# Mixed-branch diffusion step on one core: Fourier branch by even and odd halves, gate sigmoids in the z eviction, head statistics inside the mLSTM

## What is computed

```python
z = h @ w_in + b_in                    # 6672 columns: q k v o | u | g_a g_b | gates
# branch A: bidirectional mLSTM, 4 heads of 256; hsum = forward + backward
hn = (hsum - mean) * rsqrt(var + eps) * g_head          # per head and token
y_a = (sigmoid(o) * hn) @ w_a
# branch B: 4 groups of 128 channels
uf = u.reshape(B, L, 4, 128)
y_f = real(fft2(uf, axes=(1, 3), norm="ortho"))
y_b = y_f.reshape(B, L, 512) @ w_b
merged = sigmoid(g_a) * y_a + sigmoid(g_b) * y_b
x = layer_norm(ALPHA * x + gate1 * (merged @ w_out))
# then a mixture of 16 experts, top 2, and a second layer norm
```

## Times and profile before

| | |
|---|---|
| Time, median of 3 runs | 1269.01 us (1265.07 to 1269.72) |
| Profiled execution: span, first to last instruction | 1264.4 us (its time outside the span is not listed) |
| PE busy | 1124.0 us (89%) |
| PEld busy | 901.4 us (71%) |
| DVE busy | 693.0 us (55%) |
| ACT busy | 466.9 us (37%) |
| POOL busy | 168.1 us (13%) |
| DMA | 217.00 MB, mean 172 GB/s |
| Chain that ended last | PE 65%, DMA 14%, DVE 13%, ACT 4%, issue 3% |

### The profile page before, as it was taken

The page is one execution under the profiler, slowest core; times in us unless marked ns, Lnnn a source line. Parts: engine busy times, 40 slices in busy tenths (PEclk is TensorE's granted clock), DMA queues, the critical chain, the costliest instruction groups (busy, mean ns, idle before and its releaser), DMA issues.

```text
span 1264.4 us, 15216 instructions
## 1 busy us (share of the span) xinstructions
PE 1124.0 (89%) x5699; PEld 901.4 (71%) x5700; DVE 693.0 (55%) x982; ACT 466.9 (37%) x549; POOL 168.1 (13%) x126
## 2 busy tenths in 40 slices
PE   5899999999999969999989999938999999999710
PEld 1498889999999964767555558826888778778510
DVE  0499982222222224657333319762478988988548
ACT  1431222222222234217211000123478878888522
POOL 3000000000000000000001117510011221122056
PEclk9899999999999999999999999958999999999865
DMA  9644632223222521003311223324769999999542
GB/s 321 237 164 163 216 121 68 66 68 98 66 66 69 180 67 68 1 1 112 161 67 67 83 81 136 138 78 166 266 243 384 398 389 390 393 395 397 213 182 83
DMA packets 110442, 217.00 MB, mean 172 GB/s; under 512 B 3245, under 2 KB 43425, under 8 KB 110401
## 3 DMA queue, kind: packets, MB, share of 16 engines
q1 hardware_dynamic: 103221, 191.67, 42.3%
q0 software_dynamic: 4592, 15.40, 3.5%
q10 hardware_dynamic: 2592, 9.44, 1.8%
HBM read 194.95 MB, written 21.55 MB: 171 GB/s over the span
## 4 chain that ended last, share of the span: by engine, by line
PE 65%; DMA 14%; DVE 13%; ACT 4%; issue 3%; SPq 1%; POOL 0%; POOLq 0%; DVEq 0%; ACTq 0%
PE bank L895 14%; PE bank L896 13%; PE bank L897 13%; DMA z<-w_gate 11%; PE bank L1113 7%; PE bank L1056 2%; DVE g_hl L1527 2%; PE bank L1086 2%; PE bank L1038 2%; DVE z L1291 2%; PE bank L1058 2%; PE bank L1115 2%; ACT g_hl L775 2%; PE bank L886 2%; DMA r<-w_ada 2%
## 5 line engine op out<-in xcount | busy, mean ns | idle before, releaser
L895 PE MATMUL bank<-hT_hi,w_hl 128*128 128x320 f32 x832 | 258.5, 311 | 1.1 <-DVE w_hl L1247 1.1
L896 PE MATMUL bank<-hT_lo,w_hl 128*128 128x320 f32 x832 | 257.1, 309 | 0.0
L897 PE MATMUL bank<-hT_hi,w_hl 128*128 128x320 f32 x832 | 255.2, 307 | 0.0
L895 PEld LDWEIGHTS bank<-hT_hi,w_hl 128*128 128x128 f32 x832 | 156.6, 188 | 7.3 <-issue 5.2
L897 PEld LDWEIGHTS bank<-hT_hi,w_hl 128*128 128x128 f32 x832 | 156.6, 188 | 0.0
L896 PEld LDWEIGHTS bank<-hT_lo,w_hl 128*128 128x128 f32 x832 | 156.3, 188 | 0.0
L1334 DVE TENSOR_TENSOR z<-bank,cols 128x320 f32<-128x320 f32 (+1 forms) x52 | 25.3, 487 | 183.4 <-PE bank L897 183.4
L643 ACT ACTIVATE w_hl<-r 128x1024 fp32r<-128x1024 f32 x52 | 55.0, 1059 | 143.2 <-PE bank L897 143.2
L1527 DVE TENSOR_TENSOR g_hl<-z,g_hl 128x2048 fp32r<-128x2048 f32 x32 | 72.0, 2288 | 34.4 <-ACT g_hl L775 34.4
L565 POOL TENSOR_TENSOR z<-z 128x640 f32<-128x640 f32 x8 | 18.0, 2250 | 527.2 <-DVE z L1470 527.2
L1113 PE MATMUL bank<-z,r 128*128 128x512 f32 x192 | 85.1, 593 | 1.1 <-DVE z L1455 1.1
(11 more groups left out here) (287 smaller groups left out, 2053.2 us busy)
## 6 DMA issues: line engine op xcount, KB each, us to landing
z<-w_gate SPq DMA_DIRECT2D x16, 2048.0 KB, 12.0
z<-w_up SPq DMA_DIRECT2D x16, 2048.0 KB, 11.4
z<-w_down SPq DMA_DIRECT2D x16, 2048.0 KB, 11.7
r<-w_in SPq DMA_DIRECT2D x26, 1024.0 KB, 5.3
z<-w_ada SPq DMA_DIRECT2D x8, 2048.0 KB, 8.0
y_d<-r ACTq DMA_DIRECT2D x18, 512.0 KB, 6.4
r<-w_ada SPq DMA_DIRECT2D x3, 2048.0 KB, 15.6
y_d<-zeros SPq DMA_DIRECT2D x1, 4608.0 KB, 19.6
```

Of the source, the lines that this page charges most:

```text
L895: MM(dst, sta(0), mov(0), start=start, stop=False)
L896: MM(dst, sta(0), mov(1), start=False, stop=False)
L897: return MM(dst, sta(1), mov(0), start=False, stop=stop)
```

## The change

- The position transform of a real signal is even in its cosine part and odd in its sine part. The changed kernel computes the cosine part for 257 of 512 positions (`HALF`) and the sine part for 255 (`ODD`) and mirrors them after the projection with w_b, since that projection acts on channels alone. The channel transform is halved in the same way: 65 cosine and 63 sine columns per group, in one matmul of 128 columns, and the rows of w_b are folded to match (near plus far rows for the even part, far minus near for the odd one). The 64th channel of each group has rows of its own (`wb_mid`, `four_mid`, 4 partitions). The host gives w_b with the far rows in reversed order.
- PE no longer waits for the last unit outputs before the channel transform.
- In the projection to z, ACT evicts both halves of the blocks o, g_a, g_b with a sigmoid; the three sigmoid passes after the mLSTM go.
- DVE takes the statistics of a head right after its second direction (and of the context after the context part), normalises head by head, folds w_b between heads 1 and 2, and gates the transposed blocks in between.
- w_b comes as four loads of 64 partitions, the middle rows in a fifth, behind w_a. The load of x_prompt into r3 moves behind the last gating, since `yb_mix` uses its place.
- ACT copies the first 257 columns of the w_b product out of PSUM (`yb_mix`) and DVE adds and subtracts the other 255 to give both halves.
- Semaphores of the root (`var_ready`, `std_ready`) are shared by three places.

```diff
+    t128 = np.concatenate([np.cos(a[:, 0:65]), np.sin(a[:, 1:64]), np.cos(a), np.sin(a)], 1) / np.sqrt(P)
+    b = 2 * np.pi * ((np.arange(TL)[:, None] * np.arange(HALF)[None]) % TL) / TL
...
+        four_a = zf[:, 0:NT * NG * P].rearrange("p (t c g f) -> p t c g f", t=NT, g=NG, c=2)
...
+        wb_near = r1[:, 0:2048].rearrange("p (n d) -> p n d", n=2)
+        wb_far = r1[:, 2048:4096].rearrange("p (n d) -> p n d", n=2)
+        wb_even = wb_near
+        wb_spare = r1[:, 4096:5120]
+        wb_odd = [r1[:, 3072:4096], r1[:, 2048:3072]]
+        yb_mix = [r3[:, 4096 + s * 512:4608 + s * 512] for s in range(2)]
...
+            wb_rows = a["w_b"][0].rearrange("(n g f) d -> g f n d", n=2, g=2)
+            for g in range(2):
+                sp.dma_start(wb_near[64 * g:64 * g + 64, :, :], wb_rows[g, 0:64]).then_inc(wb_loaded, 16)
+                sp.dma_start(wb_far[64 * g:64 * g + 64, :, :], wb_rows[g, 64:128]).then_inc(wb_loaded, 16)
+            sp.dma_start(wa_sb, a["w_a"][0].rearrange("(k p) n -> p k n", p=P)).then_inc(wa_loaded, 16)
+            sp.wait_ge(four_a_out, NT)
+            sp.dma_start(wb_mid, a["w_b"][0].rearrange("(g f) d -> g f d", g=NG)[:, 64, :]).then_inc(four_loaded, 16)
...
+            sp.wait_ge(y_gated, KT)
             sp.dma_start(xr[:, NL, :], a["x_prompt"][0]).then_inc(xr_loaded, 16)
...
+                    if not gate:
+                        first_half.then_inc(z_out, 1)
+                    else:
+                        act.wait_ge(w_used, 4 * b + f + 1)
+                        A(z[:, bass.ds(4 * b + f, 1), TH:T].rearrange("p a t -> p (a t)"), bank[2 * (f % 2) + 1][:, 0:TH], ACT.Sigmoid,
+                          bias=cols[:, bass.ds(16 + 4 * b + f, 1)]).then_inc(z_out, 1)
...
-            for f in (ZO, ZGA, ZGB):
-                A(z[:, f:f + 8, :], z[:, f:f + 8, :], ACT.Sigmoid).then_inc(sig_ready, 1)
...
+            A(four_p[:, 0, :], bank[2][:, 0:HALF], ACT.Copy).then_inc(four_out, 1)
...
+            A(four_mid[:, :], bank[7][0:NG, 0:HALF], ACT.Copy).then_inc(four_out, 1)
...
+                A(yb_mix[m % 2][:, 0:HALF], bank[YR[m % 2]][:, 0:HALF], ACT.Copy).then_inc(yb_copied, 1)
...
+                for g in range(NG):
+                    last = MM(bank[tt % 2][:, g * P:(g + 1) * P], z[:, ZU + g, tt * P:(tt + 1) * P], t128_sb[:, 0:P], start=True, stop=True)
+                last.then_inc(four_a_mm, 1)
+            pe.wait_ge(four_a_out, NT)
+
+            def pair(s, kind, n):
+
+                return four_a[:, s, kind, 2 * n:2 * n + 2, :].rearrange("p g f -> p (g f)")
+
+            def even(dst, n):
+                for s in range(NL):
+                    last = MM(dst, pair(s, 0, n), four_l[:, 0, s, :], start=(s == 0), stop=(s == NL - 1))
+                return last
...
+            def odd(dst, n):
+                for s in range(NL):
+                    last = MM(dst, pair(s, 1, n), four_l[:, 1, s, 1:HALF - 1], start=(s == 0), stop=(s == NL - 1))
...
+            even(bank[2][:, 0:HALF], 0).then_inc(four_mm, 1)
+            odd(bank[3][:, 0:ODD], 0).then_inc(four_mm, 1)
+            even(bank[4][:, 0:HALF], 1).then_inc(four_mm, 1)
+            for n in range(2):
+                MM(bank[1][:, n * P:(n + 1) * P], pair(NL, 0, n), cos_c, start=True, stop=True)
+            for n in range(2):
+                last = MM(bank[1][:, (2 + n) * P:(3 + n) * P], pair(NL, 1, n), sin_c, start=True, stop=True)
+            last.then_inc(four_mm, 1)
...
+            odd(bank[0][:, 0:ODD], 1)
+            for n in range(2):
+                last = MM(bank[0][:, (2 + n) * P:(3 + n) * P], pair(NL, 1, n), cos_c, start=True, stop=True)
+            last.then_inc(four_mm, 1)
+            pe.wait_ge(unit_out, 30)
+            for s in range(NL):
+                last = MM(bank[7][0:NG, 0:HALF], four_a[:, s, 1, :, 0:1].rearrange("p g o -> p (g o)"), four_l[:, 0, s, :], start=(s == 0), stop=(s == NL - 1))
+            last.then_inc(four_mm, 1)
+
             pe.wait_ge(unit_out, 32)
...
+            pe.wait_ge(four_out, 8)
             TB = ((6, 7), (4, 5))
             for k in range(KT):
-                pe.wait_ge(hn_ready, 1)
+                pe.wait_ge(hn_ready, k // 2 + 1)
...
+            pe.wait_ge(wb_folded, 5)
+            pe.wait_ge(four_loaded, 48)
...
+                for n in range(2):
+                    MM(bank[bb][:, 0:HALF], wb_even[:, n, w], four_p[:, n, :], start=(n == 0), stop=False)
+                MM(bank[bb][:, 0:HALF], wb_mid[:, w], four_mid[:, :], start=False, stop=True)
+                for n in range(2):
+                    MM(bank[bb][:, HALF:TL], wb_odd[n][:, w], four_q[:, n, :], start=(n == 0), stop=(n == 1))
+                for n in range(2):
+                    MM(bank[bc][:, P:2 * P], wb_even[:, n, w], four_pc[:, n, :], start=(n == 0), stop=False)
+                for n in range(2):
+                    MM(bank[bc][:, P:2 * P], wb_odd[n][:, w], four_qc[:, n, :], start=False, stop=(n == 1))
...
+                y_b(m, bc, bb)
+                if m == 0:
+                    pe.wait_ge(wa_loaded, 16)
+                for k in range(KT):
+                    if m == 0:
+                        pe.wait_ge(yin_ready, k + 1)
+                    MM(bank[ba][:, :], wa_sb[:, k, m * P:(m + 1) * P], z[:, ZO + k, 0:TL], start=(k == 0), stop=(k == KT - 1))
...
+            def row_stats(cells):
+
+                for tt, h in cells:
+                    last = V.bn_stats(bn[:, 4 * tt + h, :], hsum[:, tt, h * HD:(h + 1) * HD])
+                then(last)
...
+            row_stats([(NL, h) for h in range(H)])
...
+                if q % 2 == 1:
+                    dve.wait_ge(unit_out, 4 * q + 4)
+                    row_stats([(tt, q // 2) for tt in range(NL)])
...
+            normed(0)
+            normed(1)
+            dve.wait_ge(wb_loaded, 16 * 4)
+            dve.wait_ge(pool_setup, 10)
+            for n in range(2):
+                V.scalar_tensor_tensor(out=wb_spare if n == 0 else wb_odd[1], in0=wb_near[:, n, :], scalar=neg_keep[:, 0:1], in1=wb_far[:, n, :], op0=ALU.mult, op1=ALU.add).then_inc(wb_folded, 1)
+                dve.wait_ge(wb_folded, 2 * n + 1)
+                V.scalar_tensor_tensor(out=wb_even[:, n, :], in0=wb_far[:, n, :], scalar=row_keep[:, 0:1], in1=wb_near[:, n, :], op0=ALU.mult, op1=ALU.add).then_inc(wb_folded, 1)
+                dve.wait_ge(wb_folded, 2 * n + 2)
+            V.tensor_copy(wb_odd[0], wb_spare).then_inc(wb_folded, 1)
+            gated(0)
+            gated(1)
+            normed(2)
+            gated(2)
+            gated(3)
+            normed(3)
+            for k in range(4, KT):
+                gated(k)
...
+                dve.wait_ge(yb_copied, m + 1)
+                V.tensor_tensor(mix[:, TL - 1:HALF - 1:-1], mix[:, 1:HALF - 1], bank[bb][:, HALF:TL], ALU.subtract).then_inc(dve_chain, 1)
+                chain[0] += 1
+                then(V.tensor_tensor(mix[:, 1:HALF - 1], mix[:, 1:HALF - 1], bank[bb][:, HALF:TL], ALU.add))
+                V.tensor_tensor(z[:, ZGA + m, 0:TL], z[:, ZGA + m, 0:TL], bank[ba][:, :], ALU.mult)
+                V.tensor_tensor(z[:, ZGA + m, TL:T], z[:, ZGA + m, TL:T], bank[bc][:, 0:P], ALU.mult)
+                V.tensor_tensor(z[:, ZGB + m, TL:T], z[:, ZGB + m, TL:T], bank[bc][:, P:2 * P], ALU.mult)
+                V.tensor_tensor(z[:, ZGB + m, 0:TL], z[:, ZGB + m, 0:TL], mix, ALU.mult).then_inc(y_gated, 1)
```

233 lines of the change are left out of this document (130 added, 103 removed).

## The result

The change takes **1251.3 us** (median of 4 runs, 1248.1 to 1252.4), the kernel before 1268.6 in the same series: ratio 0.986, 95% interval 0.984 to 0.988. The profiled execution has a span of 1249.3 us. So the change is faster, by 17 us (1.4%) where 27.8 were forecast, and its time lies outside the range of 1235.5 to 1248.

A forecast was written before the change was run, and what follows sets the result against it. TensorE was taken to bound the stretch from the mLSTM through the branch projections. First projection -18.8 (holding the statistics' +4.7), y blocks -10.3, hand-over +1.3 sum to -27.8: 1269.0 becomes 1241.2 us, range 1235.5 to 1248.

The forecast's parts named there:

- Statistics in the mLSTM, +4.7: DVE's statistics after heads 0, 1, 2 delay the mLSTM by 4.7 us; the context's four cost nothing.
- Fourier on TensorE: Halved channel and position transforms: no wait for unit outputs, channel transform 4.65 us, turns start at 616.3.
- DVE beside it: DVE's normalisations, w_b folds (6.05 us) and gating beside TensorE: folds end at 616.9, first y_b at 626.7.
- rival A: w_b's load into 64 partitions runs at half rate and lands late: folds and all behind +2.8 us, 1244.0; chance 0.27.
- The clock: TensorE behind the Fourier part was priced at full clock; a fall stood only in rivals.
- Rival C: The clock falls while TensorE only turns, 616.3 to 626.7: +1.8 us, 1243.0; chance 0.09.
- Rival D: The clock does not come back in the y blocks, 23.4 us each; with all eight 1334.8 us; chance 0.01.
- Hand-over +1.3: From the last y block to the output projection, ACT's eviction and two dependent folds come ahead: +1.3 us.
- Projections, 11.70 a block: The eight y blocks of the branch projections take 11.70 us each instead of 12.98: -10.3 us.
- Costed at nothing: Sigmoid evictions on ACT in z's projection, and later loads of x_prompt and rows behind the gating: no cost.

The follow-up runs named there:

- free_stats: The changed kernel with the statistics of heads 0, 1 and 2 one pair later in the mLSTM: 1241.6 us, 0.979 of the kernel before.
- late_stats: The changed kernel with all twenty statistics put back behind the last unit output, after the mLSTM: 1246.1 us, 0.981 of the kernel before.
- spread_rows: The changed kernel with the four w_b pieces written to every second partition, timing only, Fourier branch not the layer's: 1244.8 us, 0.981 of the kernel before.
- norm_ahead: The changed kernel with head 2's five normalisations moved ahead of the folds, into DVE's wait for w_b: 1244.5 us, 0.981 of the kernel before.
- warm_both: The changed kernel with unused extra matmuls in TensorE's waits among the turns and ahead of the output projection: 1244.4 us, 0.981 of the kernel before.
- warm_turns: The changed kernel with two unused 512-column matmuls ahead of each of the turns' three waits for the gating: 1246.1 us, 0.981 of the kernel before.
- pad_mid: The changed kernel with the middle frequency's 4-row matmul padded with zeros to 128 rows: 1245.8 us, 0.981 of the kernel before.
- late_sigmoids: The changed kernel with linear z evictions and three sigmoids on ACT ahead of the channel evictions: 1249.6 us, 0.985 of the kernel before.
- four_losses_out: The changed kernel with extra matmuls in TensorE's waits, 128 middle rows and head 2's normalisations ahead of the folds: 1238.3 us, 0.976 of the kernel before.

## Why the prediction was right and wrong

It was right that the change is faster, and on most of the mechanism, and wrong by 10 us in the size.

- *Statistics in the mLSTM, +4.7*: right. Between the score matmuls of two heads there are 26.5 and 26.6 us instead of 25.0, and behind the last head 2.1 more than in free_stats: 5.2 (5.0 against before without its wait of 1.22). That the context's four cost nothing held as well: up to head 1 late_stats, which has them elsewhere, takes 508.7 us.
- *Fourier on TensorE*: right. Channel transform 4.74 us (4.65), 16.3 us from its start to the turns (16.0). The four-column matmuls (eight recorded) took 1.91 us, the last one's end included, 0.43 each as taken.
- *DVE beside it*: normalisation started 7.3 us behind the channel transform (7.2), the folds took 5.9 (6.05). **Wrong**: "w_b lands about 609.5, before 610.8". It landed 12.4 us behind the start of the channel transform and 12.2 behind its first issue, 1.9 after DVE was ready for it. This is rival A with its first price (13 us for the load), 2.8 forecast, 1.4 measured on the path (spread_rows, norm_ahead). The mistake was to find no row for a load into 64 partitions and then take the full rate: no row spoke for that either.
- *The clock*: this is **the step that failed**. The sum prices everything behind the Fourier part at the full clock: the turns, y block 0 at 11.7 and the output projection as in before. The runs showed 8.0 us in its place (warm_both). Rival C had the chance of 0.09 and the price of 1.8 us, for the turns alone; they did run at 0.50, but most of the loss is in the dense matmuls behind. Rival D's start is there too, 7.4 us of block 0 at 0.50, but the clock came back within the block. I argued from the earlier trace rows that turns at 640 to 645 stood at 1.00. They did, but busier. Windows of before, the turns and then the hand-over, for comparison with 1.28 and 1.47 of 3 us in the change:

```profile
636.00:639.00 3.00, 1.61 (x13) 1.00 0.00 0
639.00:642.00 3.00, 2.39 (x17) 1.00 0.01 3
642.00:645.00 3.00, 2.03 (x15) 1.00 0.00 0
749.00:752.00 3.00, 1.18 (x9) 1.00 0.43 154
```

  The last row warns against reading too much into one window: TensorE was less busy there than in either window of the change, and the clock stayed. I had the gaps in hand, since I had worked out when DVE would release each turn, and did not add them up. The clock cost 3.3 us in the y blocks, all in block 0, and 0.2 to 0.6 ahead of it (warm_both, warm_turns).
- *Hand-over +1.3*: right (3.10 for 1.82). **Wrong** was that this is its whole price. Behind the longer gap the clock is at 0.50, and 14 matmuls take 0.43 us each from start to start instead of 0.23, 2.8 us, with the dip at 785 4.4; the gap of 1.82 us in before was followed by 1.00. This place was in no rival: more than the term itself stood behind it.
- *Projections, 11.70 a block*: the sum of the columns was right and **the price of one term was not**: the middle matmul was priced by its columns, and its 4 rows cost 0.40 us more per block, 3.2 in all (pad_mid). I gave the small weight load in the Fourier part (128 rows, 4 columns) a bound ("can only be shorter") and gave none here. With 8 x 1.28 the gain of the columns is 10.2, not 10.3; half the rate from 600.3 is 613.3, not 613.6. Neither changes anything.
- *Costed at nothing*: the sigmoids cost nothing (late_sigmoids). The new waits of x_prompt and the rows were not tried apart; four_losses_out's output projection of 81.9 us, as before, leaves no room for a cost. Not forecast were the 2.9 and 1.3 us gained up to head 1 (first traces, second traces), 1 of them in the wait for the start state. The rest may be scatter: in the traces of the edited kernels this part takes 506.2 to 510.7 us.

Sum: clock 8.0, rows 3.2, w_b 1.4 and the statistics' 0.3 are 12.9 of the 13.5 in the four parts; the unforeseen gain of 3 in the medians outside them leaves the 10 us.

## What to carry to other kernels

When a change leaves TensorE shorter work between the same waits, add up its idle time over every hand-over and ask what the clock will be behind it; a gap of 3 us cost another 1.5 to 2.8 in the dense matmuls that followed, and matmuls whose result nothing reads, put into the gap, took that away. Price a matmul by its columns only beside neighbours of the same number of rows, and a load by which partitions it writes and how its first dimension divides among the DMA engines. And statistics or other small work moved off the end of a stage belongs where the engine waits in the stage before, to be found in its timeline: one pair later it was free, one pair earlier it cost 5.2 us.
